# Two places where the first features are multiplied for all output tiles ahead of the rest, and a norm's inverse moved in front of a weight split

## The reference

```
mixed = concat([rms_norm(oa) * g_a, rms_norm(ob) * g_b], -1) @ w_out
x = x + gate_mix * mixed
h = modulate(rms_norm(x), shift_ffn, scale_ffn)
gate, val = split(causal_depthwise_conv(h @ w_up, conv_w, conv_b), 2, -1)
x = x + gate_ffn * ((silu(gate) * val) @ w_down)
```

## Time and profile before

| | |
|---|---|
| median of 3 runs | 1816.52 us (1815.6 to 1816.91) |
| the profiled execution, its span | 1815.0 us |
| TensorE busy | 1782.3 us (98%) |
| VectorE busy | 1096.4 us (60%) |
| ScalarE busy | 732.8 us (40%) |
| output product's second half and FFN start | about 297 to 370 us |

### The profile page before, as it was taken

How to read it: one execution, slowest core, us unless ns; L and a number is a source line. 1 busy time by engine, 2 the same in 40 slices (tenths; PEclk the granted TensorE clock), 3 DMA queues, 4 the chain that set the end, 5 groups by cost and what they waited for, 6 DMA issues and landing times.

```text
span 1815.0 us, 22458 instructions
## 1 busy us (share of the span) xinstructions
PE 1782.3 (98%) x8312; PEld 1428.5 (79%) x8312; DVE 1096.4 (60%) x1601; ACT 732.8 (40%) x1031; POOL 40.7 (2%) x78
## 2 busy tenths in 40 slices
PE   7999999999999999999999999999999999999998
PEld 6887556788888888878888888889766788888887
DVE  6977775655555335775677774245577567767423
ACT  6313664344334323444444443232365443443322
POOL 4110000000000000000000000000000000000000
PEclk9999999999999999999999999999999999999999
DMA  9793112223322323312332222323401233222231
GB/s 356 251 337 136 47 53 93 82 93 101 107 93 87 97 94 94 115 48 93 105 104 92 92 92 87 104 85 107 163 24 47 70 108 100 92 92 92 93 105 70
DMA packets 149082, 195.29 MB, mean 108 GB/s; under 512 B 3647, under 2 KB 133001, under 8 KB 146333
## 3 DMA queue, kind: packets, MB, share of 16 engines
q1 hardware_dynamic: 141272, 155.28, 26.3%
q0 software_dynamic: 7600, 39.13, 5.8%
q10 hardware_dynamic: 148, 0.05, 0.0%
HBM read 189.15 MB, written 5.29 MB: 107 GB/s over the span
## 4 chain that ended last, share of the span: by engine, by line
PE 93%; DVE 4%; ACT 1%; issue 1%; DMA 0%; SPq 0%; ACTq 0%; DVEq 0%
PE bank L809 21%; PE bank L810 21%; PE bank L811 21%; PE bank L872 3%; PE bank L874 2%; PE bank L873 2%; PE bank L1454 2%; PE bank L1452 2%; PE bank L1453 2%; PE bank L948 2%; PE bank L965 1%; PE bank L996 1%; PE bank L852 1%; PE bank L853 1%; PE bank L854 1%; PE bank L1047 1%
## 5 line engine op out<-in xcount | busy, mean ns | idle before, releaser
L1922 DVE TENSOR_TENSOR w_lo<-w_stage,w_hi 128x2048 fp32r<-128x2048 f32 (+3 forms) x135 | 296.7, 2198 | 439.6 <-ACT w_hi L1480 439.5
L809 PE MATMUL bank<-act_hi,w_hi 128*128 128x512 f32 x1232 | 482.0, 391 | 1.6 <-DVE act_lo L1972 0.7
L811 PE MATMUL bank<-act_hi,w_lo 128*128 128x512 f32 x1232 | 479.5, 389 | 0.0
L810 PE MATMUL bank<-act_lo,w_hi 128*128 128x512 f32 x1232 | 479.4, 389 | 0.0
L1480 ACT ACTIVATE w_hi<-w_stage 128x2048 fp32r<-128x2048 f32 (+3 forms) x137 | 251.7, 1837 | 456.6 <-PE bank L811 334.6
L809 PEld LDWEIGHTS bank<-act_hi,w_hi 128*128 128x128 f32 x1232 | 231.2, 188 | 53.4 <-DVE act_lo L1972 2.3
L811 PEld LDWEIGHTS bank<-act_hi,w_lo 128*128 128x128 f32 x1232 | 231.2, 188 | 48.3
L810 PEld LDWEIGHTS bank<-act_lo,w_hi 128*128 128x128 f32 x1232 | 231.3, 188 | 47.7 <-issue 0.5
L809 PE MATMUL bank<-mid_hi,w_hi 128*128 128x512 f32 x352 | 136.9, 389 | 0.0
L810 PE MATMUL bank<-mid_lo,w_hi 128*128 128x512 f32 x352 | 136.9, 389 | 0.0
L811 PE MATMUL bank<-mid_hi,w_lo 128*128 128x512 f32 x352 | 136.9, 389 | 0.0
(11 more groups left out here) (412 smaller groups left out, 2612.3 us busy)
## 6 DMA issues: line engine op xcount, KB each, us to landing
ada_stage<-in_w_ada POOLq DMA_DIRECT2D x24, 1024.0 KB, 7.2
w_stage<-in_w_up SPq DMA_DIRECT2D x22, 1024.0 KB, 5.0
w_stage<-in_a_ffn_in SPq DMA_DIRECT2D x22, 1024.0 KB, 5.1
w_stage<-in_b_ffn_in SPq DMA_DIRECT2D x22, 1024.0 KB, 5.0
w_stage<-in_w_in SPq DMA_DIRECT2D x10, 1024.0 KB, 7.3
w_stage<-in_b_ffn_out SPq DMA_DIRECT2D x10, 1024.0 KB, 5.0
w_stage<-in_w_down SPq DMA_DIRECT2D x8, 1024.0 KB, 5.0
w_stage<-in_a_ffn_out SPq DMA_DIRECT2D x8, 1024.0 KB, 5.1
```

The costliest lines, as they stand in the source:

```text
L809: pe.matmul(dst, wh, mh, start=start and k == 0, stop=False)
L810: pe.matmul(dst, wh, ml, start=False, stop=False)
L811: last = pe.matmul(dst, wl, mh, start=False, stop=stop and k == nk - 1)
L1922: dve.tensor_tensor(w_lo[slot][:, 0:n], raw[:, 0:n], w_hi[slot][:, 0:n].bitcast(FP32), ALU.subtract).then_inc(w_ready, 1)
```

## The change

At the output product, k = 4 and then k = 5 are multiplied for all four tiles of the first two chunks; then each tile gets k = 6 and 7. At the FFN, the first chunk is multiplied with k outside and its two tiles inside (`up_first`), the second chunk follows as a single call of `chunk`, and the loop of pairs starts at its second round. On VectorE, `out_phase` without `move` no longer splits chunk `C0[ph] + 5` ahead of `invert`; that split comes after the eight tiles are scaled and ahead of the copies of the memory products. ScalarE's list is not changed.

```diff
+            def up_first(c):
+
+                pe.wait_ge(w_ready, c + 1)
+                pe.wait_ge(group_free, G0["up0"] - 1)
+                for k in range(KT):
+                    for m in range(2):
+                        part(c, 0, m, [k], act, tile_wait=normed("up0") if m == 0 else None, start=k == 0,
+                             stop=k == KT - 1)
+
...
             w_out_part(1, 1, range(4), start=True)
+            for k in (4, 5):
+                for s in range(2):
+                    for m in range(2):
+                        w_out_part(s, m, [k], tile_wait=normed("w_out") if s == m == 0 else None)
             for s in range(2):
                 for m in range(2):
-                    w_out_part(s, m, range(4, 8), tile_wait=normed("w_out") if s == m == 0 else None, stop=True)
+                    w_out_part(s, m, range(6, 8), tile_wait=normed("w_out") if s == m == 0 else None, stop=True)
             gemm_pairs("w_out", 2, o_0, normed("w_out"), first=1, swap=1)
...
             mem_half(3, 1)
-            gemm_pairs("up0", FT // 2, act, normed("up0"))
+            up_first(C0["up0"])
+            chunk(C0["up0"] + 1, 1, KT, CHUNK_COLS, act, g=G0["up0"] + 1, gslot=1)
+            gemm_pairs("up0", FT // 2, act, normed("up0"), first=1)
             gemm_down(0)
...
                 after(name, 6, move)
                 after(name, 7, move)
-                split_w(C0[ph] + 5, 1)
+                if move:
+                    split_w(C0[ph] + 5, 1)
                 invert(name)
...
                         bias=lambda t: modv(SHIFT_FFN, t))
+            split_w(C0["up0"] + 1, 1)
             mem_group(2)
             mem_group(3)
             up(0)
```

## The result

| | before | after |
|---|---|---|
| median of 20 runs each, side by side | 1816.43 us (1815.6 to 1819.3) | 1819.8 us (1817.55 to 1822.82) |
| the profiled execution, its span | 1815.0 us | 1819.5 us |

The ratio is 1.0019, with a 95% interval of 1.0013 to 1.0025: slower by 3.4 us, 0.19%. Behind each median stand the lowest and the highest run. The lowest runs lie 1.95 us apart, the highest 3.5.

What follows compares the result with a forecast made beforehand. TensorE was taken as the bound, 93% of the chain of waits. The later store moved the second FFN round from 370.45 to 372.45, +2.0 us on a median of 1816.5, giving 1818.5 us, range 1816.2 to 1821.0.

Steps and rivals of the forecast that it cites:

- the forecast: Whole kernel: second FFN round 2.0 us later, median 1818.5 us; chance 0.45.
- Part 1: Output product: chunk 0 complete 1.46 us later, third chunk starts at 311.14 instead of 309.68 after some 3.0 us standing.
- Part 2: VectorE's reciprocal of the FFN norm, put ahead of the split, comes at 338.94, 0.25 us later than before.
- Part 3: First FFN chunk never waits, ends at 359.17 against 359.57; 1.86 us recovered, new tile order worth 0.47.
- Part 4: Copies 2.45 us later behind the moved split; store lands in 4.6 us beside a load; second round at 372.45.
- Store undisturbed: Ahead of the second FFN round: store lands in 2.6 us despite a load; net 0.0, 1816.5 us; chance 0.20.
- store as slow as beside two loads: At ScalarE's wait before its FFN table load: store takes 6.6 us, +4.0, 1820.5 us; chance 0.10.
- The sum: Second FFN round starts at 372.45 instead of 370.45, +2.0 us (0.0 to +4.0); the rest follows unchanged.
- the clock falls in the longer gap: At the output product's 3.0 us gap: clock falls, third chunk 1.7 us late; +3.7, 1820.2 us; chance 0.20.
- The change does all it is said to: Output product: third chunk's weights not late, gaining 1.62 instead of losing 1.46; -1.1, 1815.4 us; chance 0.05.

Runs made afterwards that it cites:

- e1: The kernel before with only the output product regrouped (k=4 and 5 for all four tiles first); 1818.28 us, ratio 1.0012.
- e7: e6 with the output product taken chunk by chunk, k outside and the chunk's two tiles inside; 1813.85 us, ratio 0.9983.
- e8: e6 with the first FFN chunk in its old tile order too, leaving only the earlier reciprocal; 1815.51 us, ratio 0.9996.
- e6: The changed kernel with the output product in its old order and the copies ahead of the moved split; 1814.17 us, ratio 0.9988.
- e5: The changed kernel with the fourth FFN weight load held back until the stores have landed; 1817.87 us, ratio 1.0007.
- e3: The changed kernel with VectorE's copies of the memory products ahead of the moved split; 1816.94 us, ratio 1.0002.
- e2: The changed kernel with the output product back in its old order; 1816.76 us, ratio 1.0006.
- e4: The changed kernel with 12 extra matmuls, result unused, filling the gap ahead of the output product's third chunk; 1819.5 us, ratio 1.0014.
- e9: e3 with the 12 extra matmuls of e4 in the output product's gap; 1815.82 us, ratio 0.9996.
- e10: e5 with the 12 extra matmuls of e4 in the output product's gap; 1816.81 us, ratio 1.0001.

## Why the prediction was partly right

It named 1818.5 us with a range of 1816.2 to 1821.0, and gave no change within 0.2% a chance of 0.77. Measured were 1819.8, inside the range, and +0.19%, inside the bound by 0.3 us, which is partly luck. The steps of order held; the choice between the forecast and the rival of the clock did not.

- **Part 1** said that chunk 0 would be complete 1.46 later and the third chunk with it, after some 3.0 us of standing. d1 grew by 1.50, the gap is 2.92, and e1 shows it alone. e7 shows the reason too: with chunk 0 complete early, the loss turns into a gain of 1.24.
- **Part 2** had the reciprocal 0.25 later. In the profiles it is 339.88 - 338.69 = 1.19 later; without the 1.61 of the clock's fall ahead of it and with the 0.69 by which this execution came earlier it is 0.27. That is a gain of 1.46 - 0.25 = 1.21 on a reciprocal left behind its split; e8 gives 1.23.
- **Part 3** had the first FFN chunk free of waits and the tile order worth 0.47. No wait shows in it, and e8 against e6 gives 0.51. Of the 1.86 us that it counted as recovered, 1.74 are (e6), mostly because the first triple behind the memory products takes 350.00 - 349.13 = 0.87 and not 0.80.
- **Part 4** had the copies 2.45 later and took 4.6 us for the store's landing, between 2.6 and 6.6. By the reckoning of part 2 the copies came 356.57 - 353.18 - 0.92 = 2.47 later; the store took 4.4. *Store undisturbed* and *store as slow as beside two loads* are both refuted, and e5 shows that the load beside it is the cause. The 4.6 was the middle of two ends that are not alike, and that it came so close is partly luck: with no load there were two stores in flight, with two loads only one.
- **The sum** for the order of work was +2.0; measured are +1.50 and +0.31, +1.81. Taken apart by the runs: +1.50 (e1), -1.23 and -0.51 (e8, e6), +2.05 (e3), in all +1.81. The last three are steps from one kernel to the next and add up by themselves; that the output product and the FFN do not act on each other is what e3 and e6 show, with a d3 of 22.00 in both.
- **The failed step is the clock's.** The prediction put *the clock falls in the longer gap* at 0.20 against the forecast's 0.45, and named a fall between 308 and 320 as what would make it wrong. It fell there in the profiled execution, at the price given: 1.7 forecast, 1.61 measured. The median is 3.37 over before, which is the order's 1.81 and 1.6 beside it, about one fall; it lies nearer to that rival's 1820.2 than to 1818.5. The working erred in three points. Its price came from 204 to 208, where the fall cost work but next to no time, since VectorE was the limit; it held for the new gap because TensorE runs back to back behind it, which the prediction did not ask. The windows of 260 to 280, at a clock of 1.00, hold their 2.7 us without work in pieces, and I let them weigh against a gap in one piece. And only one gap was priced, although the prediction itself forecast a second, at the conv taps; in the profiled execution the clock fell there too, which is all but 0.1 or 0.2 of the +1.74 behind it (1446.3 to the end against 1444.7 in e2 and e4, which have that gap and no fall). That falls come in some executions and not in others was not in the cases at all: it makes a mixture, whose top, 1822.82, lies above the range's end.
- *The change does all it is said to* is refuted by d1. e6 and e7 show what was needed for it: not to move the split ahead of the copies, and not to delay chunk 0.

How much of the time is the clock stays an estimate. In the mean the changed kernel is 3.45 over before; the order's 1.81 taken off, 1.6 are left. The pairs with and without filling give 0.9 to 1.1 of it to the first gap. The other 0.5 or so are not shown by any run; falls at the second gap, which e4 has too and e9 and e10 lack, would account for them.

## What to carry to other kernels

When an order of products is changed to hide a stall, look first at when each output tile is complete and who waits for that: work taken from later tiles hides the stall and delays the release, and a grouping by no more tiles than the release needs (e7) gave both. When a split or copy is moved on one engine, follow the loads that its buffer releases: here two lines in the other order put a load beside a store and cost 2.05 us. And a new gap of TensorE is priced with its own length and with a fall of the clock behind it, weighted, not one or the other.

## What the runs showed of the hardware

- The clock fell behind a gap of 2.92 us in three profiled executions and not in a fourth, and behind one of 1.91 us in the changed kernel but not behind 1.96 (e2) or 1.97 (e4). Each fall behind the longer gap cost 1.61 us, within 0.02. A fall cost time only where TensorE was what the rest waited for: that at 204 to 208 in the kernel before cost less than 0.1 us against e1. The Trainium skill, page "TensorE: Matmul & The Clock Gate", section "HAM oscillation — how this bites in real kernels", has a kernel in which TensorE waits some 3 to 5 us for data and then starts its next burst at half rate. The gaps here are shorter than that, and the clock fell behind them all the same in after, e3 and e5 (0.50 in the windows), though not in e1 (1.00).
- The second of two stores of 256 KB lands in 2.6 to 2.7 us without a load ahead of it (before, e3, e5) and took 4.4 to 4.5 behind one load of 1 MB on another queue (after, e2). A single store of 256 KB took 6.6 beside two such loads.
